# Where the second block's modulation is weighed and summed during the first feed-forward: DVE in place of TensorE

## The reference

```
mx = split(silu(c)     @ w_mod[l] + b_mod[l], 6)      # six vectors of 1024, for the latent stream
mc = split(silu(c_ctx) @ w_mod[l] + b_mod[l], 6)      # the same for the context stream
x = x + mx[2] * (mixers(modulate(rms_norm(x), mx[0], mx[1]) @ w_in[l]) @ w_out[l])
x = x + mx[5] * ((silu(z @ w_gate[l]) * (z @ w_up[l])) @ w_down[l])   # z = modulate(rms_norm(x), mx[3], mx[4])
```

## Time and profile before

| | us |
|---|---|
| median of 3 runs (1888.81 to 1891.89) | 1891.16 |
| profiled execution, first to last instruction (span) | 1884.1 |
| PE busy in it | 1662.6 (88%) |
| DVE busy | 699.9 (37%) |
| ACT busy | 541.2 (29%) |
| POOL busy | 516.5 (27%) |

### The profile page before, as it was taken

The page is one execution under the profiler, slowest core; times in us unless marked ns, Lnnn a source line. Parts: engine busy times, 40 slices in busy tenths (PEclk is TensorE's granted clock), DMA queues, the critical chain, the costliest instruction groups (busy, mean ns, idle before and its releaser), DMA issues.

```text
span 1884.1 us, 22935 instructions
## 1 busy us (share of the span) xinstructions
PE 1662.6 (88%) x9310; PEld 1343.1 (71%) x9310; DVE 699.9 (37%) x1108; ACT 541.2 (29%) x849; POOL 516.5 (27%) x231
## 2 busy tenths in 40 slices
PE   4789994688989999999999997996679799999998
PEld 2467774456877888888888886776447677778786
DVE  3442234663432322332223353516554422423324
ACT  3212222662252111111111125322652522222223
POOL 0712222001214322322323211333103253444431
PEclk8789997889989999999999998998799889999998
DMA  6434630000234232123332110221001224133221
GB/s 246 160 134 134 168 116 7 1 1 1 67 111 157 92 109 87 59 100 111 111 111 96 60 45 21 69 67 45 1 1 36 98 67 134 67 101 100 67 89 45
DMA packets 122192, 155.20 MB, mean 82 GB/s; under 512 B 20352, under 2 KB 89872, under 8 KB 122128
## 3 DMA queue, kind: packets, MB, share of 16 engines
q1 hardware_dynamic: 122128, 154.32, 25.3%
HBM read 152.21 MB, written 2.10 MB: 82 GB/s over the span
## 4 chain that ended last, share of the span: by engine, by line
PE 77%; DVE 11%; ACT 5%; issue 3%; SPq 2%; POOL 2%; DMA 2%; DVEq 0%; ACTq 0%; POOLq 0%
PE ps L1505 16%; PE ps L1506 15%; PE ps L1507 15%; PE ps L1801 5%; PE ps L1803 5%; PE ps L1802 5%; PE ps L1428 2%; PE ps L1687 2%; PE ps L1709 2%; DVE s_at L1274 1%; DVE hl L1367 1%; PE ps L1725 1%; PE ps L1820 1%; PE ps L1821 1%; PE ps L1822 1%
## 5 line engine op out<-in xcount | busy, mean ns | idle before, releaser
L1505 PE MATMUL ps<-zh,wh 128*128 128x512 f32 x1632 | 588.9, 361 | 32.8 <-POOL zl L445 11.2
L445 POOL TENSOR_TENSOR wl<-raw,wh 128x1024 fp32r<-128x1024 f32 x144 | 353.6, 2468 | 853.2 <-ACT wh L547 853.2
L1506 PE MATMUL ps<-zl,wh 128*128 128x512 f32 x1632 | 583.8, 358 | 0.0
L1507 PE MATMUL ps<-zh,wl 128*128 128x512 f32 x1632 | 580.0, 355 | 0.0
L1505 PEld LDWEIGHTS ps<-zh,wh 128*128 128x128 f32 x1632 | 312.2, 191 | 116.4 <-issue 42.8
L1507 PEld LDWEIGHTS ps<-zh,wl 128*128 128x128 f32 x1632 | 311.2, 191 | 45.9
L1506 PEld LDWEIGHTS ps<-zl,wh 128*128 128x128 f32 x1632 | 312.2, 191 | 42.6
L547 ACT ACTIVATE wh<-raw 128x1024 fp32r<-128x1024 f32 x144 | 148.5, 1058 | 398.3 <-PE ps L1507 280.5
L1380 DVE SCALAR_TENSOR_TENSOR xT<-ps,modcol,xT 128x512 f32<-128x512 f32 (+1 forms) x264 | 169.4, 661 | 103.8 <-PE ps L1803 100.3
L1361 DVE TENSOR_TENSOR hf<-gs,ps 128x512 f32<-128x512 f32 x66 | 37.5, 596 | 408.8 <-ACT gs L859 408.6
L1801 PE MATMUL ps<-hh,wh_d 128*128 128x512 f32 x480 | 174.0, 363 | 13.3 <-DVE xT L1380 13.2
(11 more groups left out here) (226 smaller groups left out, 1603.0 us busy)
## 6 DMA issues: line engine op xcount, KB each, us to landing
raw<-in_w_gate_dram SPq DMA_DIRECT2D x22, 1024.0 KB, 7.0
raw<-in_w_up_dram SPq DMA_DIRECT2D x22, 1024.0 KB, 9.4
raw_m<-in_w_mod_dram SPq DMA_DIRECT2D x22, 1024.0 KB, 5.1
raw_d<-in_w_down_dram SPq DMA_DIRECT2D x20, 1024.0 KB, 4.9
raw<-in_w_in_dram SPq DMA_DIRECT2D x14, 1024.0 KB, 5.4
raw<-in_w_mod_dram SPq DMA_DIRECT2D x11, 1024.0 KB, 5.2
raw_n<-in_w_mod_dram SPq DMA_DIRECT2D x9, 1024.0 KB, 5.2
raw<-in_w_out_dram SPq DMA_DIRECT2D x32, 256.0 KB, 4.4
```

What stands on the lines that cost most here:

```text
L445: nc.gpsimd.tensor_tensor(dst, src, hi.bitcast(F32), ALU.subtract).then_inc(sem(done), 1)
L1505: MM(dst, wt_h[:, h, w], zh[:, k, c0:c1], start=(k == 0), stop=False)
L1506: MM(dst, wt_h[:, h, w], zl[:, k, c0:c1], start=False, stop=False)
L1507: last = MM(dst, wt_l[:, h, w], zh[:, k, c0:c1], start=False, stop=(k == KC - 1))
```

## The change

`mod_half` is no longer called in the feed-forward of layer 0. In its place DVE runs `mod_sums(s)`: for each of the 8 slices of the panel and each of the two streams it multiplies the 128x512 slice by the partition's own number silu(c) and adds it to a 128x512 sum (`macc`, one for each stream). That is 16 instructions a step: 2 `tensor_scalar` and 14 `scalar_tensor_tensor`. Each but the first two waits for the instruction two before it (the last one on the same sum). After each half DVE waits for all its sums and raises `use_mod` with a `memset` of one column. In steps 1 to 10 this stands where `mod_copy` stood, behind `chunk_lo(s, 0)`; in step 0 it stands in front of `chunk(0, 0)`. PE's `mod_finish_sums` takes the place of `mod_finish`: 8 matmuls of a 128x128 part of `macc` with one column of ones, which sum over the partitions. It waits for all 16 sums. The wait of PE for `ev_d0` in front of the first half's matmuls goes with them.

```diff
+                def mod_sums(s):
+                    for half in range(2):
+                        dve.wait_ge(sem(f"ld_mod{6 + half}"), 16 * (s + 1))
+                        panel = (raw_m, raw_m2)[half][:, :].rearrange("p (j n) -> p j n", j=4)
+                        for j in range(4):
+                            for stream in range(2):
+                                c_col = cz[:, 4 * half + j, stream:stream + 1]
+                                if half or j:
+                                    dve.wait_ge(sem("macc_add"), 16 * s + 2 * (4 * half + j - 1) + stream + 1)
+                                    last = V.scalar_tensor_tensor(macc[:, stream, :], panel[:, j, :], c_col, macc[:, stream, :],
+                                                                  ALU.mult, ALU.add)
+                                else:
+                                    last = V.tensor_scalar(macc[:, stream, :], panel[:, j, :], c_col, None, ALU.mult)
+                                last.then_inc(sem("macc_add"), 1)
+                        dve.wait_ge(sem("macc_add"), 16 * s + 8 * half + 8)
+                        V.memset(stats[:, 0, 3 + half:4 + half], 0.0).then_inc(sem("use_mod"), 1)
 
                 def ffn_step(s, par, first=False):                       # DVE
+                    if l == 0 and first:
+                        mod_sums(s)
                     chunk(s, 0, par)
                     chunk_lo(s, 0, par)
-                    if l == 0:
-                        mod_copy(M_FFN + 2 * s + 2)
+                    if l == 0 and not first:
+                        mod_sums(s)
                     chunk(s, 1, par)
                     if l == 0:
                         mod_add(J_FFN + s)
...
+            def mod_finish_sums(s):                                       # PE
+                pe.wait_ge(sem("macc_add"), 16 * (s + 1))
+                for i in range(4):
+                    for stream in range(2):
+                        at = 256 + 2 * i + stream
+                        last = MM(ps[:, MODCOLS[0], at:at + 1], macc[:, stream, P * i:P * i + P], ones[:, 0:1], start=True, stop=True)
+                last.then_inc(sem("mod_fin"), 1)
...
                         last = three_pass(wh[0], wl[0], h, (ps[:, 3 * h, :], ps[:, 3 * h + 2, 0:SC]), l == 0)
                         last.then_inc(sem("use_a"), 1)
-                        if l == 0 and h:
-                            ffn_mod(s, 1)
                         pe.wait_ge(sem("loB"), 2 * b + h + 1)
...
                         last.then_inc(sem("use_b"), 1)
-                        if l == 0 and h == 0:
-                            pe.wait_ge(sem("ev_d0"), KC * (s - 1) + 1)
-                            ffn_mod(s, 0)
                     pe.wait_ge(sem(f"ev_h{l}"), 2 * s + 2)
                     if l == 0:
-                        mod_finish(J_FFN + s)
+                        mod_finish_sums(s)
                     down(s - 1, 1 - par)
```

More of the change, by code:

```diff
@@ L208, in slot_of @@
             return 2 * (tiles_before(n) + kk) + n + kv
-        hh, hl, gs, hf, raw_d, raw_m, wh_d, wl_d, raw_m2 = overlay([
+        hh, hl, gs, hf, raw_d, raw_m, wh_d, wl_d, raw_m2, macc = overlay([
             ("hh", [P, 2, 2, NT], F32R), ("hl", [P, 2, 2, NT], F32R), ("gs", [P, NT], F32), ("hf", [P, NT], F32),
             ("raw_d", [P, 2048], F32), ("raw_m", [P, 2048], F32), ("wh_d", [P, 2, 1024], F32R),
-            ("wl_d", [P, 2, 1024], F32R), ("raw_m2", [P, 2048], F32)])
+            ("wl_d", [P, 2, 1024], F32R), ("raw_m2", [P, 2048], F32), ("macc", [P, 2, 512], F32)])
         fz, = overlay([("fz", [P, KC, SX], F32)], under=[(n + "_f", s, d) for n, s, d in norm_bufs])
@@ L1387, in down @@
                             add_square(2 * l + 2, n - 1, W)
-                MODBANK[0], MODCOLS[0] = 6, 1
+                MODCOLS[0] = 1
+                def mod_sums(s):
[14 more added lines that the diff above has]
+                        V.memset(stats[:, 0, 3 + half:4 + half], 0.0).then_inc(sem("use_mod"), 1)
                 def ffn_step(s, par, first=False):
+                    if l == 0 and first:
+                        mod_sums(s)
                     chunk(s, 0, par)
                     chunk_lo(s, 0, par)
-                    if l == 0:
-                        mod_copy(M_FFN + 2 * s + 2)
+                    if l == 0 and not first:
+                        mod_sums(s)
                     chunk(s, 1, par)
@@ L1414, in _ @@
                     dve.wait_ge(sem("ev_dc0"), KC * FSTEPS)
-                MODBANK[0], MODCOLS[0] = 4, 7
+                MODCOLS[0] = 7
             norm(4, SX)
@@ L1779, in _ @@
                 norm(2 * l + 1, W)
-                MODBANK[0], MODCOLS[0] = 6, 1
-                def ffn_mod(s, h):
-                    mod_half(h, (raw_m, raw_m2)[h], 6 + h, s + 1)
+                MODCOLS[0] = 1
                 def down(s, par, wd_h=wh_d, wd_l=wl_d):
@@ L1824, in ffn_first @@
                                     last.then_inc(sem(("use_a", "use_b")[up]), 1)
-                    if l == 0:
-                        ffn_mod(0, 0)
-                        ffn_mod(0, 1)
                     pe.wait_ge(sem(f"ev_h{l}"), 2)
                     if l == 0:
-                        mod_finish(J_FFN)
+                        mod_finish_sums(0)
                 def ffn_step(s, par):
```

## The result

The changed kernel takes 1905.74 us (median of 4 runs, 1904.55 to 1910.62); the kernel before, run again beside it, 1889.99. The ratio is 1.0089 (95% interval 1.0070 to 1.0109): some 17 us slower. The interval stays clear of 1. The direction was forecast, the size was not: 7 us were expected.

A forecast was written before the change was run, and what follows sets the result against it. PE was taken to bound the changed stage, busy 527.95 of 530 us. Step 1's +6.5 and +3.5, loop steps' -1.5 and step 10's -1.4 gave +7 on 1891.2, hence 1898 us, range 1888 to 1918.

The forecast's parts named there:

- The saving on PE: Each step: two modulation groups removed save 2.4 us, the longer finish costs 1.0, so 1.4 us gained if nothing waits.
- The start of the sums: Loop step on DVE: sums begin when POOL's second subtraction ends, at 815.66, not after chunk_lo at 813.40.
- rival 2: Loop steps: sums start at 813.5, PE never waits, eight steps gain 1.4 us each; total 1888 or 1883 to 1885; chance 0.14.
- The length of the sums: Loop step on DVE: all 16 instructions with the turn at the middle take 10.3 us.
- their distance: DVE's scaled additions: 0.66 us start to start, with bounds 0.66 and about 0.80.
- PE's wait: Loop step, in front of the finish: PE idle 1.1 us until the sums end.
- rival 3: Every loop step: sums 0.80 apart run into POOL's next subtraction, +4.3 us a step, total 1932; chance 0.16.
- The rule that the prediction takes from the Trainium skill: DVE: next instruction waits until the pipe empties; sums 0.75 apart, a step 1.0 us slower; the prediction held trace evidence against it.
- Step 1 in sum: Step 1: late sums cut by POOL cost +6.5 us and the fallen clock +3.5 us.
- rival 1: Step 1: POOL does not get in between the sums, which end at 612.9; total +2 us, 1893; chance 0.20.
- A loop step gains nothing: Eight loop steps: PE waits for what it gave up; -0.1 us, taken as -0.2 a step, about -1.5 us.
- The prediction's own sign for rival 3: Loop steps lasting over 1 us more than the 53.7 us of before would show rival 3.

The follow-up runs named there:

- e1: Changed kernel with every step's sums moved in front of chunk(s, 0), as in step 0; 1872.72 us, 0.9911 of the kernel before.
- e4: Changed kernel with PE's finish behind the down product and, in steps 1 to 10, DVE's mod_add behind the last scaled addition; 0.9951 of the kernel before.
- e2: Changed kernel with only step 1's sums also moved in front of chunk(s, 0), steps 2 to 10 left as they were; 1.0031 of the kernel before.
- e5: Changed kernel with five useless dense 512-column matmuls on PE before the wait for the sums in steps 1 to 10; 1.0043 of the kernel before.
- e3: Changed kernel with the finish done for the latent stream alone (4 matmuls, 8 records), the context stream's left out; 0.9964 of the kernel before.
- e6: e1 with each step's finish done twice (32 one-column records); 1.0135 of the kernel before.

## Why the prediction was right and wrong

**What held.** The saving on PE: in step 10, where nothing waits, -1.5 us were measured and -1.4 forecast; e1 and e4, without waits, gain 1.48 and 1.56 in each loop step. The start of the sums: POOL's subtraction came first and held them to its end, so rival 2 fell. The Trainium skill ("SBUF — State Buffer", SBUF: two separate sides) describes this as a lock on a port pair shared by the two, held for a whole instruction; the rows agree (the first `tensor_scalar`, issued at 830.47, ended 0.3 us after POOL). The length of the sums (10.2 for 10.3), their distance (0.66), and with it PE's wait (1.0 for 1.1): rival 3 fell. The rule that the prediction takes from the Trainium skill ("VectorE: DVE Perf Modes", The DRAIN you can't avoid) does not fit here either: eight sums of 0.74 us took 5.39. Step 1 in sum: +10.1 for +10.0, with POOL between the sums, so rival 1 fell, and e2 shows that it was all in the place of the sums. That it came out to 0.1 us is partly luck. The sums ended 0.6 us earlier than forecast, and the finish behind them lost 1.7 us to the clock where 1 was charged. PE was 1.6 us less ahead than forecast, because a dip came behind step 0's finish too (clock 0.50 from 580 to 582), so its idleness was 8.1 us in place of 10; that costs nothing, since the last sum sets when PE goes on.

**The step that failed** is "A loop step gains nothing (-0.1; ... 8 steps: about -1.5 us)". Its working was right as far as it went: e2's one step without a dip and e5 lasted 53.30 and 53.34 us, 0.4 under before, even a little better than forecast. A term was missing, or put at nothing without a reason. I charged the clock for step 1's 10 us of idleness and never asked what a wait of 1 us followed by a finish of one-column matmuls does. The finish was priced by its length alone. The dip costs 1.54 us in seven of eight steps and 3.1 in one, together 13.9 us. Less the 1.8 us by which eight steps without a dip (-0.4 each) are better than the -1.5 us forecast for them, that is 12.1 us, just what the loop missed (+10.6 measured, -1.5 forecast). e3 (fewer records), e4 and e1 (no wait) and e5 (wait filled) each take the dip away with another handle, and e6 brings it back with no wait at all. The prediction's own sign for rival 3, loop steps longer by over 1 us, did come (+1.32), and not by rival 3: the sums stood 0.66 apart and ended before POOL asked.

**Smaller errors.** The 7.1 us that I put outside the span were mostly the scatter of the runs. In the changed kernel's profiled run 1910.62 - 1908.8 = 1.8 us lie outside; by the same 1.8 the profiled run of before took about 1885.9, one of its faster ones. The clock did not "still" stand at 0.50 at 535 to 540; in between it had risen, with PE hardly at work:

```profile
530.00:535.00 5.00, 0.33 (x3) 0.10 (x1) 2.99 (x4) 3.71 (x7) 2.64 (x2) 0.84 0.18 43
```

The upper bound of the sums adds up to 12.2 us and not 12.4, and rival 3's +35 in eight steps comes to 1935 us and not 1932. None of this moves the forecast.

**What stays open** is why the dips are of two lengths, 1.54 and 3.1 us in cost, and what decides whether one comes. Idleness and sparse matmuls add up, but their sum alone does not settle it. Some 2.4 us of the two, finish first and idleness behind it, brought a dip in step 0 of e1 (1.84 + 0.57) and of e3 (0.95 + 1.45); 3.0 us brought none in step 0 of the kernel before, nor in one of the eight loop steps of e2. No run here varied what could tell.

## What to carry to other kernels

When work is moved from the engine that bounds a kernel, look for the place where the receiving engine is idle with margin, not for the place where the old code stood: the same 16 instructions made this kernel 0.9% slower behind `chunk_lo` and 0.9% faster in front of `chunk`, where 17 us lay free. Price a wait of TensorE, and any run of one-column matmuls, by its length and by what it may do to the clock of the dense work behind it; the two add up. When a forecast gain is a balance of two near-equal terms, as 11.5 us free against 10.3 needed, look first for what can shift either of them, as POOL's subtraction did here by 2.3 us.

## What the runs showed of the hardware

- TensorE's clock fell to 0.50 after 1.0 us of idleness and 1.9 us of one-column fp32 matmuls (all eight loop steps of the changed kernel, seven of eight in e2), and within a run of 32 such records (3.8 us at the full clock) without idleness (e6); it stayed at 1.00 after the same wait with half the matmuls (e3), after the 16 records without the wait (loop steps of e1, e4), and after them with the wait filled by five 512-column matmuls (e5).
- A fall of the clock costs more than it looks: 3.4 us at half clock, 1.54 us of time, against the 1.0 us of the wait that set it off.
- DVE and POOL cut into each other instruction by instruction: six sums that take 4.05 us alone took 8.34 beside POOL, two of them recorded for 2.9 in place of 0.74, and POOL's own two subtractions grew from 4.75 to 5.20 (e1).
- Sums that each wait for the instruction two before them run 0.66 us apart, as do such instructions with no wait among them.
